# The squares of a two-tile latent rank: added on GpSimd, then summed over partitions by one TensorE product

## The reference

```python
MLA_Q_LORA = 256
def rms_norm(x, g):
    xf = x.astype(jnp.float32)
    y = xf * lax.rsqrt(jnp.mean(xf * xf, axis=-1, keepdims=True) + EPS)
    return (y * g.astype(jnp.float32)).astype(x.dtype)
...
    h = rms_norm(x, norm_g)
    proj = h @ w_in
...
    q_b = (rms_norm(c_q, q_norm_g) @ w_uq).reshape(B, S, MLA_HEADS, MLA_NOPE + MLA_ROPE)
...
for l in range(DEPTH):      # DEPTH = 2
    x = hybrid_layer(x, ...)
```

## Time and profile before

| what | value |
|---|---|
| median of 3 runs | 1286.33 us |
| lowest and highest | 1285.38 and 1287.37 us |
| the profiled execution | 1287.24 us |
| its span, first to last instruction | 1285.2 us |
| mean granted clock of TensorE | 0.998 of full speed |
| busy: TensorE, VectorE, ScalarE, GpSimd | 97%, 60%, 46%, 19% |

### The profile page before, as it was taken

The page is one execution under the profiler, slowest core; times in us unless marked ns, Lnnn a source line. Parts: engine busy times, 40 slices in busy tenths (PEclk is TensorE's granted clock), DMA queues, the critical chain, the costliest instruction groups (busy, mean ns, idle before and its releaser), DMA issues.

```text
span 1285.2 us, 17838 instructions
## 1 busy us (share of the span) xinstructions
PE 1240.4 (97%) x6498; PEld 949.7 (74%) x6498; DVE 769.3 (60%) x1599; ACT 596.3 (46%) x1109; POOL 249.3 (19%) x373
## 2 busy tenths in 40 slices
PE   5999999999999999999999999999989999999998
PEld 5777666665678888888887776665657888888887
DVE  5988777887743343444556477887874424434442
ACT  4457656765752232233245365676666323223330
POOL 1373111365710000000000021125673000000000
PEclk9999999999999999999999999999999999999999
DMA  7345112201423323333332312220133322332321
GB/s 225 96 136 132 34 33 50 66 2 54 145 66 117 93 88 97 98 98 98 98 99 67 98 33 67 49 66 1 42 94 96 114 93 89 112 93 92 98 98 66
DMA packets 122582, 109.06 MB, mean 85 GB/s; under 512 B 38784, under 2 KB 105472, under 8 KB 122496
## 3 DMA queue, kind: packets, MB, share of 16 engines
q1 hardware_dynamic: 122496, 107.93, 28.3%
HBM read 100.57 MB, written 7.34 MB: 84 GB/s over the span
## 4 chain that ended last, share of the span: by engine, by line
PE 75%; DVE 11%; ACT 6%; issue 3%; POOL 2%; SPq 1%; DMA 1%; DVEq 0%; ACTq 0%; POOLq 0%
PE bank L882 20%; PE bank L884 20%; PE bank L883 20%; DVE w_lo L760 3%; PE bank L1201 2%; PE bank L1218 2%; PE bank L1028 2%; PE bank L1234 2%; PE bank L838 1%; PE bank L1052 1%; PE bank L1247 1%; DVE score L1953 1%; PE bank L1207 1%; PE bank L1069 1%; ACT soft L1532 1%
## 5 line engine op out<-in xcount | busy, mean ns | idle before, releaser
L882 PE MATMUL bank<-h_hi,w_hi 128*128 128x512 f32 (+1 forms) x928 | 362.1, 390 | 7.8 <-DVE w_lo L760 5.4
L884 PE MATMUL bank<-h_hi,w_lo 128*128 128x512 f32 (+1 forms) x928 | 352.6, 380 | 0.0
L883 PE MATMUL bank<-h_lo,w_hi 128*128 128x512 f32 (+1 forms) x928 | 352.5, 380 | 0.0
L760 DVE TENSOR_TENSOR w_lo<-raw,w_hi 128x2048 fp32r<-128x2048 f32 (+2 forms) x98 | 188.3, 1923 | 124.0 <-ACT w_hi L754 123.9
L882 PEld LDWEIGHTS bank<-h_hi,w_hi 128*128 128x128 f32 x928 | 175.5, 189 | 59.4 <-issue 16.9
L754 ACT CAST w_hi<-raw 128x2048 fp32r<-128x2048 f32 (+2 forms) x100 | 159.0, 1594 | 113.5 <-PE bank L884 110.1
L884 PEld LDWEIGHTS bank<-h_hi,w_lo 128*128 128x128 f32 x928 | 175.6, 189 | 33.5
L883 PEld LDWEIGHTS bank<-h_lo,w_hi 128*128 128x128 f32 x928 | 175.7, 189 | 32.1 <-issue 1.9
L1729 ACT ACTIVATE gate<-bank,gains 128x512 f32<-128x512 f32 x48 | 33.0, 688 | 166.3 <-PE bank L884 166.2
L1649 ACT ACTIVATE probs<-probs,stat 128x128 f32<-128x128 f32 (+3 forms) x128 | 71.4, 559 | 48.8 <-DVE stat L2119 32.5
L2359 POOL TENSOR_SCALAR probs<-probs,stat 128x128 f32<-128x128 f32 (+3 forms) x128 | 76.0, 598 | 65.0 <-DVE stat L2098 63.8
(11 more groups left out here) (247 smaller groups left out, 2136.4 us busy)
## 6 DMA issues: line engine op xcount, KB each, us to landing
raw<-in_w_in SPq DMA_DIRECT2D x56, 1024.0 KB, 5.2
raw<-in_w_branch SPq DMA_DIRECT2D x12, 1024.0 KB, 5.2
raw<-in_w_out SPq DMA_DIRECT2D x8, 1024.0 KB, 5.2
bias<-bias_dram SPq DMA_DIRECT2D x16, 256.0 KB, 2.9
bias<-bias_dram SPq DMA_DIRECT2D x16, 192.0 KB, 2.5
x_sb<-in_x SPq DMA_DIRECT2D x4, 512.0 KB, 6.0
bias_dram<-bias_out SPq DMA_DIRECT2D x8, 256.0 KB, 2.9
raw<-in_w_in SPq DMA_DIRECT2D x4, 512.0 KB, 4.9
```

Source lines behind the costliest of these rows:

```text
L760: e.tensor_tensor(w_lo[:, s % RING, a:b], raw[:, s % RAW, a:b], w_hi[:, s % RING, a:b].bitcast(F32), ALU.subtract).then_inc(*lo_signal(nam ...
L882: pe.matmul(out_ap, lh, rh, start=start and i == 0, stop=False)
L883: pe.matmul(out_ap, lh, rl, start=False, stop=False)
L884: mm = pe.matmul(out_ap, ll, rh, start=False, stop=stop and i == n - 1)
```

## The change

In step 12 TensorE's product of the squares of `c_q0` goes. ScalarE writes the squares of `c_q1` in step 13 into `norm_rs` instead of `norm_sq`, where those of `c_q0` still lie; it waits for VectorE's norm of `ds_q1`, the last reader of `norm_rs`, no longer for a product. GpSimd then adds the two into `norm_sq`, in step 13 behind `mask_probs(12)` and ahead of the masks of the softplus of step 13. TensorE's one product, at the place of the second, waits for that addition.

```diff
                 def norm_tile(tile):
 
+                    if tile == "c_q0":
+                        return
                     k = NORMED.index(tile)
                     if tile == "ds_q0":
                         pe.wait_ge(*dve_evac.at("ds_v"))
                     elif tile == LAST_NORM:
                         pe.wait_ge(*stick_prob.at(N_STICK - 3))
-                    elif k and tile != "c_q1":
-                        pe.wait_ge(*act_evac.at(NORMED[k - 1] + "ln"))
-                    pe.wait_ge(*act_evac.at(tile + "sq"))
-                    if tile == "c_q0":
-                        norm(tile, ones, norm_sq, True, False)
-                    elif tile == "c_q1":
-                        norm(tile, ones, norm_sq, False, True)
-                    elif tile == "ds_k":
+                    elif k:
+                        pe.wait_ge(*act_evac.at(NORMED[k - (2 if tile == "c_q1" else 1)] + "ln"))
+                    if tile == "c_q1":
+                        pe.wait_ge(*pool_work.at("c_q squares"))
+                    else:
+                        pe.wait_ge(*act_evac.at(tile + "sq"))
+                    if tile == "ds_k":
                         norm(tile, ones, norm_sq, k=HD)
                     else:
-                        norm(tile, ones if tile == "c_kv" else per_head, norm_sq)
+                        norm(tile, ones if tile in ("c_kv", "c_q1") else per_head, norm_sq)
...
                     k = NORMED.index(tile)
-                    if k:
+                    if tile == "c_q1":
+                        e.wait_ge(*dve_evac.at("ds_q1"))
+                    elif k:
                         e.wait_ge(*norm_sum.at(NORMED[k - 1]))
                     r = slice(0, HD if tile == "ds_k" else P)
-                    e.activation(norm_sq[r, :], dbank(tile)[r, :], ACT.Square).then_inc(*act_evac.tick(tile + "sq"))
+                    dst = norm_rs if tile == "c_q1" else norm_sq
+                    e.activation(dst[r, :], dbank(tile)[r, :], ACT.Square).then_inc(*act_evac.tick(tile + "sq"))
...
                 for i in range(STEPS + 1):
                     if i % ST == 1:
                         mask_probs(i - 1)
+                    if NORM_AT.get(i) == "c_q1":
+                        e.wait_ge(*act_evac.at("c_q1sq"))
+                        e.tensor_tensor(norm_sq[:, :], norm_sq[:, :], norm_rs[:, :], ALU.add).then_inc(*pool_work.tick("c_q squares"))
```

## The result

The changed kernel takes 1288.39 us, median of 14 runs (1286.33 to 1289.95). The kernel before took 1285.22 us in the same comparison, median of 14 runs (1282.63 to 1287.37). The ratio is 1.0025, 95% interval 1.0018 to 1.0033: 3.2 us slower (2.3 to 4.2). It was compared three more times, beside the experiments: 1.0034 (1.0022 to 1.0046), 1.0025 (1.0016 to 1.0033) and 1.0026 (1.0016 to 1.0035). So the change costs a little over 0.2%. Two single runs on record, one of the kernel before beside the experiments and one of e3, took over 4200 us; the ratios leave them out.

What follows compares the result with a forecast made beforehand. TensorE, busy 97% of the span, was taken to bound the kernel. Its net lateness of 1.26 us per layer, 2 x 1.26 = 2.5 us, on the 1286.33 us median gave 1288.8 us, range 1286.7 to 1292.1 us.

Steps and rivals of the forecast that it cites:

- likeliest sign: Whole kernel, against a 0.2% bound: slower got 0.55, the same 0.43, faster 0.02.
- The removed product: Step 12: without this product TensorE's projection behind it starts earlier, a gain of 0.85 us per layer.
- The chain exponentials, masks, addition, product: Step 13: the addition queues behind late masks, TensorE idles 2.2 us and the product starts 1.39 us later.
- ScalarE's Ln: Step 13: Ln of the sum starts 0.7 us late; in step 15 ScalarE takes over the full 1.4.
- The slack of 0.14 us: Stage's end, values of step 14: TensorE's existing wait for GpSimd's masks leaves it 1.26 us late.
- Nothing gives it back: Behind the stage: dependent work has no slack, so 1.26 us per layer stays, 2.5 us over both layers.
- The clock: Rival, chance 0.32: clock falls behind TensorE's new wait, 1.6 us per fall, 1290.4 us with one, 1292.0 with two.
- The reading of layer 2: Where layer 1's clock fell after two waits, layer 2 stayed at 1.00, so a fall doesn't come every time.
- The starting point: Whole kernel: the median of 1286.33 us for the kernel before, to which 2.5 us was added.
- GpSimd held up by VectorE: Rival, chance 0.06: beside VectorE the addition in step 13 stretches to 4.7 us, 3.4 more per layer, 1295.6 us.
- Absorbed: Rival, chance 0.12: a later stretch paced by VectorE or ScalarE takes back most delay, 0 to 1 us stays, 1286.8 us.
- The gain comes through: Rival, chance 0.06: the addition runs beside step 13's suffix sums, TensorE keeps 0.85 us twice, 1284.6 us.

Runs made afterwards that it cites:

- e3: Kernel before without TensorE's product of the squares of c_q0 and with no addition in its place (first tile left out of the sum): 1282.77 us, ratio 0.9980.
- e2: Changed kernel with GpSimd's addition ahead of the masks of step 12's probabilities instead of behind them: 1283.07 us, ratio 0.9983 to the kernel before.
- e5: Changed kernel with the addition on VectorE, right behind the clip of step 13, instead of on GpSimd: 1282.80 us, ratio 0.9983 to the kernel before.
- e7: Changed kernel plus two superfluous TensorE products filling the wait for GpSimd's addition: 1286.63 us, ratio 1.0015 to the kernel before.
- e4: Changed kernel with two GpSimd additions in a row instead of one, same computed result: 1291.75 us, ratio 1.0051 to the kernel before.
- e6: Changed kernel with TensorE's one product moved behind the projected half of step 13: 1287.04 us, ratio 1.0018 to the kernel before.
- e1: The changed kernel run again with nothing altered, compared with the kernel before: 1290.09 us, ratio 1.0034.
- e8: The changed kernel a third time with nothing altered, compared with the kernel before: 1287.89 us, ratio 1.0025.
- e10: The changed kernel a fourth time with nothing altered, compared with the kernel before: 1288.05 us, ratio 1.0026.
- e9: Repeat of e7, the changed kernel with two superfluous TensorE products in the wait: 1285.19 us, ratio 1.0011 to the kernel before.

## Why the prediction was right

The predicted 1288.8 us lie 0.4 us above the measured 1288.39, inside what the interval of the ratio leaves (1287.5 to 1289.5), and slower was the likeliest sign. Term by term:

- **The removed product**: predicted 0.85 us for each layer, 0.87 measured at line 883, and 0.9 in e2, e3 and e5. Right.
- **The chain exponentials, masks, addition, product**: it came in this order. The addition started 0.03 us ahead of the end of the masks' row. It took 1.26 us, a little less than the shortest of the earlier trace rows; the product followed 0.15 us behind it, where I took 0.06 from the earlier trace rows. The errors cancel: TensorE's wait is 2.08 us and the product 1.33 late where I had 2.2 and 1.39.
- **ScalarE's Ln** 0.7 us late: 0.63 (219.62 against 219.75, with 0.76 ahead). It took over TensorE's full lateness in step 15, as predicted; it waits 2.46 us there where it waited 1.76.
- **The slack of 0.14 us** at the values of step 14: there the lateness falls from 1.36 to 1.21 (I had 1.26), and TensorE is the last: the masks are done at 238.32, the product starts at 238.50, 0.33 behind the projection, at TensorE's own pace.
- **Nothing gives it back**: true but for 0.1 us. The addition of the keys' squares took 1.31 us in place of the 1.40 of the earlier trace rows. That isn't scatter: this first of the four additions takes 1.31 us in both layers of all seven traces in which the sum of `c_q` comes late through the wait, and 1.40 to 1.43 in both layers of the five others. In the kernel before it starts 0.25 us ahead of the end of a VectorE instruction with both inputs in SBUF (`q_head<-q_head,q_rs`), in the changed one 0.16 ahead. Behind it the lateness stays, read best where no other difference comes between: 1.02 us at 260 us and 0.99 at 700 in e7, and 1.09 at 880 us and 1.05 at 1270 in the changed kernel. In layer 1 the changed kernel's distance does shrink, from 1.12 to 0.50, between 315 and 319 us, but only because the kernel before has its fall there (1.6 us) and the changed one a slow VectorE addition (1.0 us, last section). The mis-sized term is this one: 1.26 us a layer by my sum, 1.12 in the trace, 0.05 of it at the product and 0.09 here; 2.5 us against 2.2.
- **The clock** as a rival was the step that was framed wrongly. I held "falls" against "doesn't fall", with 0.32, as if one of them would hold for the kernel. It is a thing of the single execution: three of eight waits. The price of one fall was right (1.6 us, 1.4 to 1.65 measured), but the sum set it against a kernel before without falls, although show one of its own. What is added to the median is about 1 us, not none or 1.6 or 3.2. The reading of layer 2 was right, though the row ends where the place begins: from 936 to 941 us the granted clock of the kernel before is 1.00 as well. The Trainium skill (TensorE: Matmul & The Clock Gate, section HAM oscillation) has a wait that is long enough put TensorE back to the lower clock, so that the work behind it starts slow. Here the length of the wait alone doesn't decide: behind one and the same 2.08 us the traces show the lower clock three times and the full clock five times.
- **The starting point** was 1.1 us high: 1286.33 us was the median of three runs, 1285.22 that of fourteen. Forecast was +2.5 us, measured +3.2, and the 2.2 us of the wait with about 1 us of the clock make up that. The time came out closer than the difference because the two errors, a start 1.1 us high and a difference 0.7 us short, have opposite signs; that is luck.
- **GpSimd held up by VectorE** didn't happen: the addition took 1.26 to 1.27 us in all eight cases. **Absorbed** didn't happen either. **The gain comes through** is what e2 is: I gave it 1.7 us with the addition beside the suffix sums, and it gives 1.8 in the trace. The reading that its inputs allow it, and that only the list forbids it, was right.

## What to carry to other kernels

An instruction that is added to an idle engine can cost more than it takes: if the instructions ahead of it in that engine's list wait for the engine that you want to serve, their wait and its own time are both paid (the changed kernel, e4). Put it where its inputs come, ahead of such work, and it can be free (e2). Here that is one exchange of two statements: e2, and likewise e5, is 0.17% faster than the kernel before and 0.4% faster than the changed one. A wait that is taken out by moving the waiting work later has to be followed along the chain behind that work too, since e6 lost by it as much as the wait had cost. And a new wait of TensorE of some 2 us should be priced with a fall of the clock in a part of the executions, less the falls that the kernel has anyway.

## What the hardware showed that I had not expected

**The busy wait.** That two superfluous products of TensorE make a kernel faster in both comparisons (1.0015 against 1.0025, 1.0011 against 1.0026) I would not have expected before the traces showed the falls. In all twelve traces at most one stretch at half speed stands between start and end. In the four with a fall behind the long wait (e1, e4, e8, e10) there is none near 315 us, where the kernel before has one. Counted over whole traces, falls are no rarer without the long wait: four of the five traces of kernels that have no long wait at this place hold one, and four of the five with an idle wait of 2 us or more. Five traces against five are too few to see what the averages of all runs show. Why a fall comes at one of these places in one execution and at another in the next stays open.

**Two additions that shut each other out.** Single executions scatter by about 1 us in each layer at a place that has nothing to do with the change, the handover from the MLA stage to the sparse attention. There VectorE and GpSimd each add a mask to a bias, both with both inputs in SBUF. The timeline of the kernel before, layer 2:

```profile
936.75 1.72 DVE L808 TENSOR_TENSOR bias<-bias,chosen 128x512 f32<-128x512 f32 x1
...
936.77 1.16 POOL L808 TENSOR_TENSOR bias<-bias,chosen 128x512 f32<-128x512 f32 x1
...
939.23 0.29 PE L1234 MATMUL bank<-probs_even,v_b 128*64 128x128 f32 x1 [0.91 <-DVE probs_odd L2106]
```

The same in e1:

```profile
938.20 0.69 DVE L808 TENSOR_TENSOR bias<-bias,chosen 128x512 f32<-128x512 f32 x1
...
938.22 1.69 POOL L808 TENSOR_TENSOR bias<-bias,chosen 128x512 f32<-128x512 f32 x1
```

The rows start 0.02 us apart in both. In the first GpSimd takes 1.16 us and VectorE 1.0 us longer than otherwise, and TensorE waits 0.91 us for what VectorE does next; in the second VectorE takes its 0.69, GpSimd 0.5 us longer, and that wait is gone. The distance between the two traces moves by 1.0 us there (from +1.45 at 934 us to +0.47 at 945). The Trainium skill (SBUF — State Buffer, section Who interferes with whom) has VectorE's second port shared with GpSimd behind an exclusive lock; both traces agree with it, and they add that which engine wins isn't fixed, though VectorE's row starts first in both. In layer 1 the same place is at 316 us: the slow VectorE row costs 1.0 us there in the changed kernel, e1, e3 and e6, and is not there in e4, e8, e9 and e10. Whoever compares single traces of this kernel has to take this place out first, as the tables here do.
